# A hybrid decoder layer on one core: three reorderings where the mixer gives way to the FFN

## What is computed

```python
def reference(x, mix_norm, w_in, ..., w_out, ffn_norm, w_ffn_gate, w_ffn_up, w_ffn_down):
    for l in range(DEPTH):
        h = rms_norm(x, mix_norm[l])
        x = x + hybrid_mixer(h, w_in[l], ..., w_branch[l], w_out[l])
        h = rms_norm(x, ffn_norm[l])
        x = x + swiglu_ffn(h, w_ffn_gate[l], w_ffn_up[l], w_ffn_down[l])
    return x

def hybrid_mixer(h, w_in, ...):
    z = h @ w_in                        # split among four mixers and their gates
    ...                                 # sparse attention, pooling, gMLP, stick-breaking attention
    merged = jnp.sum(gate.astype(proj.dtype) * proj, axis=2)
    return merged @ w_out

def swiglu_ffn(h, w_gate, w_up, w_down):
    return (jax.nn.silu(h @ w_gate) * (h @ w_up)) @ w_down
```

## Time and profile before

| | us |
|---|---|
| median of 3 runs | 811.23 |
| lowest, highest | 810.91, 812.0 |
| the profiled execution, time | 811.23 |
| its span, first to last instruction | 809.3 |

### The profile page before, as it was taken

One profiled execution on the slowest core, in us unless ns is written; L12 is line 12 of the kernel. 1 busy time (PEld: TensorE's weight loads), 2 busy tenths in 40 slices (PEclk: granted clock), 3 DMA queues, 4 the chain that ended last, 5 costly groups with the idle time before them and its releaser, 6 DMA issues.

```text
span 809.3 us, 11519 instructions
## 1 busy us (share of the span) xinstructions
PE 789.0 (97%) x4713; PEld 692.5 (86%) x4713; DVE 502.2 (62%) x743; ACT 375.8 (46%) x525; POOL 59.3 (7%) x71
## 2 busy tenths in 40 slices
PE   3999999999999999999989999999999999999998
PEld 3899887877778878878878889999988899999886
DVE  5535987656577566361284699888633478887331
ACT  5435544577845533522233465555521245554210
POOL 6000040000000050050060000000000000000000
PEclk9999999999999999999999999999999999999999
DMA  8452213121122313513314213333232233333321
GB/s 256 123 164 67 92 53 104 53 96 62 53 59 97 104 53 104 208 54 104 104 53 150 85 53 122 111 110 111 101 125 91 74 97 104 106 104 104 120 89 52
DMA packets 63763, 80.36 MB, mean 99 GB/s; under 512 B 1684, under 2 KB 51936, under 8 KB 63712
## 3 DMA queue, kind: packets, MB, share of 16 engines
q1 hardware_dynamic: 63376, 79.18, 30.6%
q0 software_dynamic: 336, 0.46, 0.2%
HBM read 75.96 MB, written 2.10 MB: 96 GB/s over the span
## 4 chain that ended last, share of the span: by engine, by line
PE 78%; issue 13%; POOL 3%; DVE 3%; ACT 1%; DMA 1%; SPq 0%; POOLq 0%; DVEq 0%
PE bank L1378 16%; PE bank L1380 16%; PE bank L1379 16%; PE bank L1745 8%; PE bank L1747 8%; PE bank L1746 8%; POOL merged L483 3%; PE bank L1544 1%; PE bank L1553 1%; DMA x_sb<-in_x_dram 1%; DVE w_lo L863 1%; PE bank L1484 1%; PE bank L1458 0%; PE bank L1528 0%; ACT h_hi L527 0%
## 5 line engine op out<-in xcount | busy, mean ns | idle before, releaser
L863 DVE TENSOR_TENSOR w_lo<-raw,w_hi 128x2048 fp32r<-128x2048 f32 (+1 forms) x45 | 100.2, 2228 | 121.1 <-ACT w_hi L503 120.8
L1378 PE MATMUL bank<-h_hi,w_hi 128*128 128x512 f32 (+1 forms) x392 | 150.7, 385 | 0.7 <-DVE h_lo L1186 0.5
L1380 PE MATMUL bank<-h_hi,w_lo 128*128 128x512 f32 (+1 forms) x392 | 149.3, 381 | 0.0
L1379 PE MATMUL bank<-h_lo,w_hi 128*128 128x512 f32 (+1 forms) x392 | 149.1, 380 | 0.0
L503 ACT ACTIVATE w_hi<-raw 128x2048 fp32r<-128x2048 f32 (+1 forms) x49 | 91.1, 1861 | 89.0 <-PE bank L1380 88.1
L1745 PE MATMUL bank<-t_hi,w_hi 128*128 128x256 f32 x320 | 89.7, 280 | 0.0
L1746 PE MATMUL bank<-t_lo,w_hi 128*128 128x256 f32 x320 | 89.3, 279 | 0.0
L1747 PE MATMUL bank<-t_hi,w_lo 128*128 128x256 f32 x320 | 89.3, 279 | 0.0
L1378 PEld LDWEIGHTS bank<-h_hi,w_hi 128*128 128x128 f32 x392 | 73.7, 188 | 15.4 <-issue 1.3
L1380 PEld LDWEIGHTS bank<-h_hi,w_lo 128*128 128x128 f32 x392 | 73.7, 188 | 14.3
L1379 PEld LDWEIGHTS bank<-h_lo,w_hi 128*128 128x128 f32 x392 | 73.7, 188 | 13.6
(11 more groups left out here) (232 smaller groups left out, 1473.5 us busy)
## 6 DMA issues: line engine op xcount, KB each, us to landing
raw<-in_w_in_dram SPq DMA_DIRECT2D x26, 1024.0 KB, 5.2
raw<-in_w_ffn_gate_dram SPq DMA_DIRECT2D x11, 1024.0 KB, 5.3
raw<-in_w_ffn_up_dram SPq DMA_DIRECT2D x11, 1024.0 KB, 5.3
raw<-in_w_ffn_down_dram SPq DMA_DIRECT2D x10, 1024.0 KB, 5.0
raw<-in_w_branch_dram SPq DMA_DIRECT2D x4, 1024.0 KB, 4.8
raw<-in_w_out_dram SPq DMA_DIRECT2D x4, 1024.0 KB, 5.1
x_sb<-in_x_dram SPq DMA_DIRECT2D x4, 512.0 KB, 5.0
x_sb<-in_x_dram SPq DMA_DIRECT2D x1, 2048.0 KB, 10.5
```

The lines of the kernel that those rows point to most:

```text
L863: vec.tensor_tensor(w_lo[:, at], raw[:, c % 2, 0:n], w_hi[:, at].bitcast(F32), ALU.subtract)\
L1378: mm(dst, l_hi, r_hi, start=start, stop=False)
L1379: mm(dst, l_hi, r_lo, start=False, stop=False)
L1380: return mm(dst, l_lo, r_hi, start=False, stop=stop)
```

## The change

Three places are reordered. No instruction is added or removed on any engine.

1. ACT, in the passage: `h2_copy(1)` stands ahead of `take_root` of tile 3 instead of behind it, and the split of chunk 36 stands ahead of `h2_high(2)` and `h2_high(3)` instead of behind them.
2. PE, in the first half of chunk 35: `turn_h2(3)` stands behind the last step (j = 1, k = 7) instead of behind k = 4.
3. ACT and DVE in the first Winograd chunk alone (m = 0). ACT: step 0 of `split_ahead` stands behind the copy L830 instead of ahead of it, and steps 1 to 3 stand behind `hidden_high` instead of ahead of it. DVE: `sums_ahead` stands behind the seed `c21_seeded` and behind `hidden`, instead of ahead of both; all four steps of low parts stand ahead of the seed `c22_ready`, instead of two ahead and two behind; `hidden_low` stands behind that seed instead of ahead of it.

```diff
@@ the scalar engine's list @@
             square(TT + 3)
+            h2_copy(1)
             take_root(slice(3, 4))
-            h2_copy(1)
+            split(PLAIN[1])
             h2_high(2)
             h2_high(3)
-            split(PLAIN[1])
...
-                split_ahead(c + 1, 0)
+                if m > 0:
+                    split_ahead(c + 1, 0)
                 act.wait_ge(S["product_done"], 7 * m + 2)
...
                 nact.activation(seventh[:, up, :], last[:, T1ST], ACT.Copy).then_inc(S["seventh_copied"], 1)
-                split_ahead(c + 1, 1, 2, 3)
                 if m == 0:
+                    split_ahead(c + 1, 0)
                     for j in range(CT):
                         hidden_high(0, j, j + 1)
+                split_ahead(c + 1, 1, 2, 3)
                 act.wait_ge(S["product_done"], 7 * m + 5)
@@ the vector engine's list @@
-                sums_ahead(c + 1)
+                if m > 0:
+                    sums_ahead(c + 1)
                 dve.wait_ge(S["product_done"], 7 * m + 3)
...
                     for j in range(CT):
                         dve.wait_ge(filled, fill_at[PLAIN[1]] + j + 1)
                         hidden(0, j, bank[(fill_at[PLAIN[1]] + j) % 2])
-                    split_ahead(c + 1, 0, 1)
-                    for j in range(CT):
-                        hidden_low(0, j, j + 1)
-                else:
-                    split_ahead(c + 1, 0, 1, 2, 3)
+                    sums_ahead(c + 1)
+                split_ahead(c + 1, 0, 1, 2, 3)
                 dve.wait_ge(S["product_done"], 7 * m + 6)
                 dve.wait_ge(S["c12_seeded"], m + 1)
                 vec.tensor_tensor(f1[:, T2ND], first[:, T1ST], seventh[:, up, :], ALU.add).then_inc(S["c22_ready"], 1)
                 if m == 0:
-                    split_ahead(c + 1, 2, 3)
+                    for j in range(CT):
+                        hidden_low(0, j, j + 1)
@@ the tensor engine's list @@
                         if (half, j, k) == (0, 1, 0):
                             turn_h2(2)
-                        elif (half, j, k) == (0, 1, 4):
+                        elif (half, j, k) == (0, 1, 7):
                             turn_h2(3)
```

## The result

| | before | changed |
|---|---|---|
| median, us | 811.51 (6 runs, 810.91 to 812.62) | 816.41 (6 runs, 815.13 to 816.78) |
| ratio | | 1.0057, 95% interval 1.0045 to 1.007 |
| profiled execution: time, span | 811.23, 809.3 | 815.86, 813.9 |

The account below looks back on a forecast made before the run. PE, busy 789.0 of 809.3 us, was taken to bound the kernel. 1.08 + 1.70 + 0.10 + 1.06 + 0.10 = 4.04 us on the profiled 811.23 gave 815.3 us, bounds 814.1 to 816.2, range with rival 2 814.1 to 816.8.

Parts of the forecast that it names:

- Part 1: Chunk 35: turn_h2(3) three steps later leaves nothing covering the 2.61 us from transposes to restart; +1.08 us.
- Part 2: ACT's order in the passage: later steps stay covered and chunk 36's early split gains nothing; 0 us.
- First stall: First Winograd chunk: P7 waits for ACT's seed c12_seeded, behind splits needing late sums; +1.70 us and 0.10 for restart.
- Second stall: P3 of m = 1 waits for seed c11_seeded, behind SiLU that waits for hidden_low; +1.06 us and 0.10 for restart.
- rival 2: DVE's backlog lives on and m = 2 or 3 stalls again; +1.2 to 1.5 us, 816.5 to 816.8; chance 0.11.
- Its end sets the sum: DVE's chain from P3 of m = 0 to P3 of m = 1, independent of the first stall, sets the total.
- Rival 1: The m = 0 reorder is covered, c12_seeded being there at 496.04; only 1.08 us left, 812.3; chance 0.06.
- Rival 3: Granted clock falls to half for one Winograd chunk, doubling its 10 us; 825; chance 0.01.

Follow-up runs that it names:

- e2: Only turn_h2(3) moved behind k = 7, against the kernel before; length from PE's first transposes to DVE's last sum 1.08 us over before, ratio 1.0012.
- e1: Only ACT's order in the passage changed, against the kernel before; length from PE's first transposes to DVE's last sum -0.01 us over before, ratio 0.9993.
- e5: Whole change, but in m = 0 ACT makes the seed c12_seeded ahead of steps 2 and 3 of chunk 38; ratio to the kernel before 1.0059.
- e9: Whole change, but DVE's four sums for chunk 38 stand ahead of the seed c21_seeded again; ratio to the kernel before 1.0024.
- e10b: e5 with each of the pair's two low parts in m = 0 made three times on DVE; ratio to the kernel before 1.0112.
- the two repeats: The whole change, unaltered, measured twice more against the kernel before; ratios 1.0058 and 1.0045.
- e7: e5 plus, in m = 0, DVE's hidden_low behind step 1 and steps 2 and 3 behind the seed c22_ready; ratio to the kernel before 1.0041.
- e8b: Kernel before with turn_h2(3) one step earlier, behind k = 3; length from PE's first transposes to DVE's last sum -0.35 us over before, ratio 0.9996.

## Why the prediction was right

Point by point, in the prediction's own steps:

- *Part 1, transposes, +1.08.* e2 gave 1.08. The step held because it is a difference of two starts in one chain of one trace: the 2.61 us from transposes to restart were 2.61 again.
- *Part 2, ACT's order, 0.* e1 gave -0.01. One sentence was put too narrowly: that DVE's split "starts at 470.6 again" is true only with the late transposes. Alone, the early split brings DVE 1.08 us, which PE has no use for.
- *First stall, +1.70 and 0.10.* P7 would have started at 494.96 + 0.62 + 1.08 = 496.66 and started at 498.38: 1.72. The recorded wait is 1.55, shorter than the loss, because a matmul's recorded end lies behind the start of the next.
- *Second stall, +1.06 and 0.10.* P3 of m = 1 started at 503.79; the prediction had 503.2 + 0.62 = 503.8. PE's later starts were 4.0 later, as forecast (P7 of m = 1 at 504.95 before and 509.57 now, less 0.62), and no further wait of PE is new; rival 2, the backlog that lives on, did not come.
- *"Its end sets the sum."* e5 showed it: with the first stall removed PE waited as much longer at the second.
- *Rival 1*, that the reorder is covered, would have needed the sums 1.7 us earlier. e9 put the third sum 4.7 us earlier (490.73 - 454.82 against 495.33 - 454.72) and PE's wait there was still 0.8, since ACT's splits stood behind `hidden_high`. So this rival's condition was incomplete as well.
- *Rival 3, the clock,* had a chance of 0.01 and rested on a gap of 2.0 us that had left the clock alone. The changed kernel's profiled execution had 1.00 at all these places. But e5 suggests that it was nearer than I had put it: a wait of 2.4 us, not much longer than those 2.0, had the clock at 0.50 behind it in the trace, and two of four executions had the lower mean. Its price was mis-sized too: 10 us for a Winograd chunk at half clock, where e5 measured 1.3 us and e10b 1.4.
- *The time.* 815.3 against a median of 816.41. The trace's length grew by 4.00, forecast 4.04. What the medians show above that, 0.9 us, is within the interval of the ratio, and the ratios of the two repeats, 1.0058 and 1.0045, lie on both sides of the forecast's 1.0050.

## What to carry to other kernels

On an in-order engine the worst place for work that is ready is behind a wait that isn't, if a neighbour will need the work soon after; here 2.5 us of sums behind a wait of 3.1 cost the kernel 1.9 us, on an engine that is busy for only 62% of the span. When several stalls lie on one chain, mending one moves the loss to the next, as e5 and e7 did: ask what sets the end of the chain, and mend its start. And work whose result passes through other engines before PE can go on (transposes, high part, low part) belongs as early as its input allows, with PE's independent work behind it and not ahead: three steps later cost 1.08 us (e2), one step earlier gave 0.35 in the trace (e8b).

## What the runs showed of the hardware that I had not expected

Behind a wait of 2.43 us (e5) and one of 5.33 us (e10b) the granted clock was 0.50, and it was back at 1.00 3.1 and 3.2 us after PE went on. In e5's trace it fell 2.1 us into the wait, in e10b's only 5.1 us into it, so the length of the wait alone does not say when. The Trainium skill ("TensorE: Matmul & The Clock Gate", section "HAM oscillation — how this bites in real kernels") tells of idle waits of TensorE behind which the next work starts at the low clock, and these two traces agree. Executions of one program differ here: e5's times were 817.69 twice, with a mean clock of 0.997, beside 815.47 and 815.73, with 1.000 and 0.999. At half clock a matmul of 256 columns had a pitch of 0.21 us against 0.12 at full clock, 1.8 times and not twice.
